# A two-layer sequence-model trunk: input handed over transposed too, the state-space input made channel by channel, its matrices and phases on VectorE

## What is computed

```python
h = x @ w_in
cq, ckv, k_rope, g_mla, u, g_s5 = split(h, (256, 128, 32, 512, 256, 256))
o_mla = mla_attention(cq, ckv, k_rope, pos, ...) * silu(g_mla)
o_s5 = s5_layer(u, ...) * silu(g_s5)
x = layer_norm(alpha * x + concat(o_mla, o_s5) @ w_out)
```

## Time and profile before

| | us |
|---|---|
| runs | 980.0, 981.01, 981.46 |
| median | 981.01 |
| profiled execution, span from first to last instruction | 978.8 |
| TensorE busy (matmul) in the span | 935.0 |
| VectorE, ScalarE, GpSimd busy | 457.3, 274.2, 275.9 |
| start of the first transposition of latents (cT) | 188.87 |

### The profile page before, as it was taken

How to read it: one execution, slowest core, us unless ns; L and a number is a source line. 1 busy time by engine, 2 the same in 40 slices (tenths; PEclk the granted TensorE clock), 3 DMA queues, 4 the chain that set the end, 5 groups by cost and what they waited for, 6 DMA issues and landing times. The chain is left out here.

```text
span 978.8 us, 12195 instructions
## 1 busy us (share of the span) xinstructions
PE 935.0 (96%) x4568; PEld 733.2 (75%) x4568; DVE 457.3 (47%) x764; ACT 274.2 (28%) x532; POOL 275.9 (28%) x278
## 2 busy tenths in 40 slices
PE   7997999799999999999999999999999999999995
PEld 5787899757677777784445477888888888888884
DVE  4539459993566569854443042310000023655453
ACT  4330510365333333431111344400110215222120
POOL 2018008433111110052344323013333343034233
PEclk9998999899999999999999899999999999999998
DMA  6501110233000000043221211011101233112111
GB/s 215 115 10 27 31 33 11 65 69 132 1 2 1 1 2 1 1 130 107 86 86 57 95 43 44 1 54 54 44 11 43 54 129 108 44 44 77 54 44 65
DMA packets 38874, 53.54 MB, mean 55 GB/s; under 512 B 15232, under 2 KB 24704, under 8 KB 38800
## 3 DMA queue, kind: packets, MB, share of 16 engines
q1 hardware_dynamic: 38816, 52.76, 17.6%
HBM read 42.72 MB, written 8.39 MB: 52 GB/s over the span
## 5 line engine op out<-in xcount | busy, mean ns | idle before, releaser
L1555 DVE SCALAR_TENSOR_TENSOR w_out_lo<-w_out_raw,gla_c,w_out_hi 128x1024 fp32r<-128x1024 f32 x8 | 10.3, 1285 | 161.9 <-ACT w_out_hi L1180 161.8
L1868 PEld LDWEIGHTS psum<-V,probT 128*128 128x128 f32 x576 | 69.3, 192 | 11.7 <-issue 8.1
L1868 PE MATMUL psum<-V,probT 128*128 128x64 f32 x576 | 74.4, 275 | 0.3 <-DVE rot L1502 0.3
L1727 PE MATMUL psum<-kT,qTt 96*128 96x512 f32 (+3 forms) x192 | 72.4, 487 | 0.0
L1112 ACT ACTIVATE prob<-psum,negmax 128x128 f32<-128x128 f32 (+7 forms) x64 | 47.4, 741 | 81.7 <-DVE negmax L1457 71.2
L1457 DVE TENSOR_REDUCE negmax<-psum 128x1 f32<-128x128 f32 (+7 forms) x64 | 48.5, 757 | 29.0 <-PE psum L1731 27.5
L1622 PE MATMUL psum<-w_out,OT 128*128 128x512 f32 x128 | 57.6, 593 | 0.0
L1622 PE MATMUL psum<-x1T_hi,wqk_hi 128*128 128x512 f32 x128 | 51.3, 401 | 0.0
L1622 PE MATMUL psum<-x1T_hi,wqk_lo 128*128 128x512 f32 x128 | 50.8, 397 | 0.0
L1622 PE MATMUL psum<-x1T_lo,wqk_hi 128*128 128x512 f32 x128 | 50.8, 397 | 0.0
L1622 PE MATMUL psum<-w_out_hi,Y1T_hi 128*128 128x512 f32 x128 | 50.6, 395 | 0.0
(11 more groups left out here) (365 smaller groups left out, 2115.9 us busy)
## 6 DMA issues: line engine op xcount, KB each, us to landing
x_ring<-x_dram SPq DMA_DIRECT2D x8, 512.0 KB, 5.4
wqk_raw<-odd_w_in_dram SPq DMA_DIRECT2D x8, 512.0 KB, 5.3
x_res<-x_dram SPq DMA_DIRECT2D x8, 512.0 KB, 3.4
x_scratch<-zn SPq DMA_DIRECT2D x8, 512.0 KB, 2.7
wv_raw<-odd_w_in_dram SPq DMA_DIRECT2D x16, 256.0 KB, 2.7
wg_raw<-odd_w_in_dram SPq DMA_DIRECT2D x16, 256.0 KB, 2.6
w_out_raw<-odd_w_out_dram SPq DMA_DIRECT2D x4, 1024.0 KB, 5.1
V<-x_scratch SPq DMA_DIRECT2D x8, 512.0 KB, 4.0
```

What stands on the lines that cost most here:

```text
L1555: step(vec.scalar_tensor_tensor(w_out1[2][:, k, :], w_out1[0][:, k, :], gla_c[:, 4 + k % 2:5 + k % 2], w_out1[1][:, k, :].bitcast(F32), AL ...
L1727: mm = pe.matmul(psum[:, slot + part, 0:c1 - c0], qTt[:, i % 2, h, :], kT[:, h, c0:c1], start=True, stop=not diag, skip_group_check=diag)
L1868: mm = pe.matmul(bank("o", i)[:, h * VD:(h + 1) * VD], lhsT, rhs, start=(k == 0), stop=(k == len(pairs) - 1))
```

## The change

- The host hands x over a second time as features by tokens (`x_cols`), and the small parameters in the layouts in which they are used (`pos_cols`, `vec_cols`, `s5_rows`, `s5_skip`). TensorE's transpositions of x, "par" and "crow" are gone; x is loaded in eight feature rows of 512 KB (the first in two halves), each split by ScalarE and VectorE in SBUF.
- "ug" becomes two blocks of 256 columns, "u" and "gs", one after the other. u is made channel-major, with 128 weight columns stationary and 512 tokens moving, as gs was. ScalarE copies it out by position t, two DMAs store it to a DRAM scratch tensor, and eight DMAs read it back as UT. SyncE waits for the store between them.
- Both halves of `phases` are run by VectorE, right after the first latents slices; ScalarE's sines come before slices 3 to 7 of "ina". VectorE makes NX and N2 itself, after the keys' rotation. GpSimd has none of this any more.
- VectorE's and ScalarE's lists are reordered to suit; the banks' ring no longer has par, crow and UT.

The diff, cut to its core:

```diff
-        wug = [split_pair(f"wug{s}", o, [P, 512]) for s, o in enumerate((D6, D6 + 1024, D3, D3 + 1024))]
-        xT_lo_parts = [at(f"xT_lo{n}", o, [P, b - a, S], F32R) for n, (a, b, o) in enumerate(
-            ((0, 2, RB + 7424), (2, 4, D4), (4, 7, D2), (7, 8, RB + 9472)))]
-        xT_lo = [t[:, k, :] for t in xT_lo_parts for k in range(t.shape[1])]
+        wu = [split_pair(f"wu{s}", D6 + 512 * s, [P, W5]) for s in range(4)]
+        wgs = [split_pair(f"wgs{s}", D3 + 512 * s, [P, W5]) for s in range(4)]
+        xT_at = (RB + 7424, RB + 8448, D4, D4 + 1024, D2, D2 + 1024, D2 + 2048, RB + 9472)
+        xT_raw = [at(f"xT_raw{k}", o, [P, S]) for k, o in enumerate(xT_at)]
...
+            ("rows", [P, 3 * G + 4 * G * GS], F32), ("dts", [P, 3, G], F32), ("dti", [P, G], I32),
...
+            ("u_rows", [P, 2, LC, NC5], F32),
...
+        u_dram = nc.dram_tensor("u_scratch", [W5, LC, NC5], F32, kind="Internal")
+        u_chunks = u_dram.ap() if not isinstance(u_dram, bass.AP) else u_dram
...
-        EARLY = 3
-        X_LAG = 2
-        for i in range(NT + X_LAG):
-            if i < NT:
-                plan.give(("xT", i, 0), 6 if i < NT - 1 else 7)
-                plan.give(("xT", i, 1), 7)
-            if i >= X_LAG:
-                plan.give(("gate0", i - X_LAG), i - X_LAG)
-        ring("par")
-        ring("crow")
+        for i in range(NT):
+            ring("gate0", i)
         for i in range(NT):
             ring("ina", i)
-        for j in range(4):
-            ring("inu", j)
+        for m in range(2):
+            for n in range(2):
+                ring("inu", m, n)
         for m in range(2):
             for n in range(2):
                 ring("ings", m, n)
         def middle_steps():
-            for q in range(4):
-                yield "UT", q
             for i in range(NT):
                 yield "cT", i
...
+            def small():
+                sp.dma_start(rows[:, :], s5_rows).then_inc(s5_loaded, 16)
+                sp.dma_start(Dt[:, :], s5_skip).then_inc(skip_loaded, 16)
+                sp.dma_start(pos_i[:, :], pos_cols).then_inc(small_loaded, 16)
+                sp.dma_start(vecs[:, :], vec_cols).then_inc(small_loaded, 16)
                 sp.dma_start(gk2[:, :], gla_w_gk2[0]).then_inc(small_loaded, 16)
...
-            for i in range(NT):
-                if i >= 4:
-                    plan.filled(sp, ("xT", i - 4, 1))
-                sp.dma_start(x_ring[:, i % 4, :], x[0, i * P:(i + 1) * P, :]).then_inc(x_loaded[i % 4], 16)
-                if i < EARLY:
-                    slice_load("gate0", i)
-                if i == 3:
-                    parameters()
-            for n in range(EARLY, 7):
-                plan.filled(sp, ("xT", n + 1, 1))
-                slice_load("gate0", n)
-            matrices()
+            for k in range(KD):
+                if k < 7:
+                    slice_load("gate0", k)
+                for half in range(2 if k == 0 else 1):
+                    s = slice(half * 512, (half + 1) * 512 if k == 0 else S)
+                    sp.dma_start(xT_raw[k][:, s], x_cols[k * P:(k + 1) * P, s]).then_inc(x_loaded[k + half if k == 0 else k + 1], 16)
+                if k == 2:
+                    small()
+            slice_load("gate0", 7)
             for n in range(3):
                 slice_load("ina", n)
-            vectors()
-            slice_load("gate0", 7)
-            for n in range(2):
-                slice_load("ug", n)
+            for n in range(4):
+                slice_load("u", n)
             for n in range(3, KD):
                 slice_load("ina", n)
             await_slice(sp, "ina", KD - 1)
-            for n in range(2, KD):
-                slice_load("ug", n)
-            await_slice(sp, "ug", KD - 1)
+            for n in range(4):
+                slice_load("gs", n)
+            for n in range(4, KD):
+                slice_load("u", n)
+            for m in range(2):
+                for n in range(2):
+                    plan.drained(sp, ("inu", m, n))
+                sp.dma_start(u_chunks[m * P:(m + 1) * P, :, :], u_rows[:, m, :, :]).then_inc(u_stored, 16)
+            slice_load("gs", 4)
+            sp.wait_ge(u_stored, 32)
+            for t in range(LC):
+                sp.dma_start(UT[t * GS:(t + 1) * GS, :, :],
+                             u_chunks[:, t, :].rearrange("(g h) c -> h g c", g=G)).then_inc(u_turned, 16)
+            for n in range(5, KD):
+                slice_load("gs", n)
+            await_slice(sp, "gs", KD - 1)
...
-            pool.wait_ge(s5_turns_set, 1)
-            phases(pool, step, 0, rot[:, :, :].rearrange("p a b -> p (a b)")[:, 0:8 * NTAB])
-            pool.wait_ge(s5_powers_set, 1)
-            for q in range(4):
-                matrix_part(pool, step, rot[:, 1:3, :].rearrange("p a b -> p (a b)")[:, 0:4 * (LC + 1) * GS], q, NX,
-                            LC + 1, LR[:, :, :], CA, LI[:, :, :], CB, ALU.subtract, s5_nx_set)
-            for q in range(4):
-                matrix_part(pool, step, rot[:, 2, :], q, N2, LC, LR[:, :, 1:LC + 1], CB, LI[:, :, 1:LC + 1], CA,
-                            ALU.add, s5_n2_set)
...
-            for i in range(NT):
+            for k in range(KD):
+                if k < 7:
+                    slice_hi("gate0", k)
                 for half in range(2):
-                    plan.filled(act, ("xT", i, half))
-                    step(act.activation(xT_hi[:, 4 * half:4 * half + 4, i * P:(i + 1) * P],
-                                        bank("xT", i, half).rearrange("p (k t) -> p k t", k=4), ACT.Copy), xT_hi_set)
-                if i < EARLY:
-                    slice_hi("gate0", i)
-            for n in range(EARLY, 6):
-                slice_hi("gate0", n)
+                    s = slice(half * 512, (half + 1) * 512)
+                    act.wait_ge(x_loaded[half if k == 0 else k + 1], 16)
+                    step(act.activation(xT_hi[:, k, s], xT_raw[k][:, s], ACT.Copy), xT_hi_set)
+            slice_hi("gate0", 7)
             for n in range(3):
                 slice_hi("ina", n)
-            for n in range(6, KD):
-                slice_hi("gate0", n)
+            for n in range(4):
+                slice_hi("u", n)
             for i in range(NT):
                 plan.filled(act, ("gate0", i))
...
+            act.wait_ge(s5_phase_set, 2)
+            step(act.activation(tabB[:, :, :], tabA[:, :, :], ACT.Sin, scale=-2 * PI_BELOW))
+            step(act.activation(tabA[:, :, :], tabA[:, :, :], ACT.Sin, scale=PI_BELOW), s5_sin_set)
...
+            for i in range(NT):
                 squares(act, step, i)
-            slice_hi("ug", 2)
-            for i in range(4, NT):
-                squares(act, step, i)
-            slice_hi("ug", 3)
             step(act.activation(stat[:, 16:24], stat[:, 0:8], ACT.Sqrt, bias=eps[:, 1:2], scale=1.0 / RQ))
             step(act.activation(stat[:, 24:32], stat[:, 8:16], ACT.Sqrt, bias=eps[:, 1:2], scale=1.0 / RKV),
                  squares_done)
+            for n in range(4):
+                slice_hi("gs", n)
             for n in range(4, KD):
-                slice_hi("ug", n)
-            for j in range(4):
-                plan.filled(act, ("inu", j))
-                step.frees(act.activation(U[:, :, 2 * j:2 * j + 2, :],
-                                          bank("inu", j).rearrange("p (t g h) -> p g t h", t=2, g=G), ACT.Copy),
-                           ("inu", j))
+                slice_hi("u", n)
+            for m in range(2):
+                for n in range(2):
+                    plan.filled(act, ("inu", m, n))
+                    step.frees(act.activation(u_rows[:, m, :, n * NC5 // 2:(n + 1) * NC5 // 2],
+                                              bank("inu", m, n).rearrange("p (c t) -> p t c", t=LC), ACT.Copy),
+                               ("inu", m, n))
+            for n in range(4, KD):
+                slice_hi("gs", n)
...
+            beside = {2: time_steps, 3: turns_of_steps, 4: magnitudes}
+            for k in range(KD):
+                if k < 7:
+                    slice_lo("gate0", k)
+                x_lo(k)
+                if k in beside:
+                    beside[k]()
+            slice_lo("gate0", 7)
             for n in range(3):
                 slice_lo("ina", n)
...
+            for half in range(2):
+                phases(vec, step, 8 * half, rot[:, :, :].rearrange("p a b -> p (a b)")[:, 0:8 * NTAB])
+            step(vec.tensor_scalar(CA, CA, sign[:, 1:2], None, ALU.mult))
+            for n in range(4):
+                slice_lo("u", n)
...
+            def make_nx(q):
+                matrix_part(vec, step, rot[:, 1:3, :].rearrange("p a b -> p (a b)")[:, 0:4 * (LC + 1) * GS], q, NX,
+                            LC + 1, LR[:, :, :], CA, LI[:, :, :], CB, ALU.subtract, s5_nx_set)
+            def make_n2(q):
+                matrix_part(vec, step, rot[:, 2, :], q, N2, LC, LR[:, :, 1:LC + 1], CB, LI[:, :, 1:LC + 1], CA,
```

(84 more changed lines are left out.)

275 lines of the change are left out of this document (103 added, 172 removed).

## The result

The changed kernel takes 926.13 us (median of 4 runs, 923.94 to 926.6) against 981.24 for the kernel before (4 runs, 980.0 to 981.74): a ratio of 0.944, 95% interval 0.943 to 0.946, or 55.1 us less. The forecast was 925. The profiled execution took 926.22 with a span of 924.5, so the time around the span is 1.7 us, where the prediction had put 2.2.

A forecast was written before the change was run, and what follows sets the result against it. TensorE, busy 96% of the span, bounds the kernel, with VectorE's sum meeting it before cT. 53.9 us less up to cT plus 2.0 after, 55.9 off 981.0, gives 925; range 919 to 934, chance 0.68.

The forecast's parts named there:

- u channel by channel: u stage on TensorE: 12 products of 512 columns instead of 24 of 256, 2.75 instead of 5.70 us a slice, 24 us less.
- rival of 949: u products keep their time because columns alone count, so the edit saves nothing there: 949 us, chance 0.01.
- Start: Without x's transpositions, TensorE's first product at 5.9 us, twelve slow products, gate products to 51.8, where the latents begin.
- Latents: Latents' projection: 192 products of 0.19 us, end 88.3; 8.4 us of waits and 3.5 after them go, 0.5 kept.
- The cover that the text called thin: Latents: after ScalarE's two sines slice 3 is split near 64, wanted at 65.4, a margin of 1 to 2 us.
- u and gs: Both stages on TensorE: 22 us each, end 132.3, plus 2 us of small waits: 134.3.
- The sum by VectorE: Up to cT: VectorE starts at 96.1, 35.7 us of instructions without pause to 131.8, last gs slice 2.75: 134.6.
- Bounce: u's DRAM store and read-back: done by 126, v wants it about 144; delays gs slice 5, costing one microsecond, bounds 0 and 9.
- signs that the prediction had listed as wrong: VectorE over 0.5 us per 256 elements, TensorE waiting on gs 5-7 behind a DMA, latents' clock 0.5, cT after 145.
- VectorE's price: Subtraction-sized VectorE instruction of 256 elements: 0.43 us with GpSimd idle; rival that slow rows are its own: 992 us, chance 0.03.
- After cT: Turned bank ring: 2.9 us less from kp's start to y, 0.9 more as first scores share banks with yT; net -2.0.
- Everything from the attention on is untouched: From the attention to the kernel's end: no change in time beyond the net -2.0 before it.

The follow-up runs named there:

- all three edits: Changed kernel with gs 5-7 loads before u's reads, M's last four steps and latents' halves earlier, u's slice 4 split ahead of gs 0-3: 919.41 us.
- second order of banks: Version with all three edits, the five banks that kp and vp take in turn reordered to 7, 4, 5, 6, 0: 919.4 us.
- the ring turned back: Changed kernel with four turns of the PSUM bank ring passed over before cT, so later jobs have the banks of the kernel before: 929.12 us.
- loads first: Changed kernel with SyncE issuing the loads of gs slices 5 to 7 before it waits for the stored u and reads it back: 924.67 us.
- M early: Changed kernel with the last four steps of M moved into VectorE's pause while ScalarE takes the squares: 925.29 us.
- latents forward: Changed kernel with latents' slice 3 split on ScalarE before the long sines and low halves from slice 4 on one place earlier on VectorE: 925.94 us.
- all of u cut: Changed kernel with all eight u slices as 24 products of 256 columns, the 512 moving tokens cut into 256 + 256: 930.44 us.
- GpSimd at work again: Changed kernel with the 24 instructions that make NX and N2 given back to GpSimd, beside VectorE: 948.05 us.

## Why the prediction was right, and where not

- **u channel by channel, 24 us:** right in size (slices of 2.74 us, 22.6 us in all with 0.5 of waits), wrong in its reason. The prediction reads "12 of them instead of 24", and takes 0.238 for 256 columns as the price of a product of that size. The runs show 0.12 for that size; 0.238 is the price of a stationary operand read with a stride of eight floats. The row was right and could not tell count, size and stride apart, because in the kernel before they came together: the reason failed, and it was luck that the sum did not need it. The rival of 949 failed because the stride went, not because columns don't count.
- **Start:** 6.17 for 5.9, the latents at 51.53 for 51.8; the slow start ended at 9.72, after eight products instead of twelve. (The 45 small instructions at 0.35 would be 16 us, not 12; both fit in the 25.)
- **Latents:** the step that failed is "I keep 0.5" for stalls: 2.5 was measured. Nor is the 0.5 in the sum: 88.3 is 51.8 and 36.5, the products alone. The cover that the text called thin was thinner: ScalarE's sines ran to 64.9 and slice 3's low half came at 65.63, slice 4's, behind the doubling of the table as named, at 71.94. Moving both forward took the waits away.
- **u and gs:** "2 us of small waits" were 2.7 (0.5 and 2.2), and the total of 47.1 stands beside 46.7. But "From here VectorE has no pause" failed: it stood 1.73 us for slice 5. The sum by VectorE explains where cT went: the start was 98.1 for 96.1 (2.0 late, with the latents), the pause added 1.7, the instructions took 35.0 instead of 35.7 (0.43, 0.76 and 0.69 each, as priced), and so the last low half was done at 134.85 for 131.8.
- **Bounce:** priced at one microsecond, and its removal gave 1.3 at cT, at the place that was named: slice 5 behind the eight reads, 128.6 for "near 127". Its parts were off and cancelled, which is luck: issuing the eight took 3.8 us, not 7; the slowest took 8.0 to land, not 3.5. This wait is one of the signs that the prediction had listed as wrong (TensorE waiting on gs slices 5 to 7 with a DMA behind it); of its signs for right, stalls under 2 us in the latents did not come either.
- **VectorE's price:** 0.43 undisturbed, as taken, and 1.16 to 1.40 with GpSimd beside it, as the rows said.
- **After cT:** 2.87 less up to y and 0.85 more up to glu, for 2.9 and 0.9.
- **"Everything from the attention on is untouched":** not quite. At glu the kernel was 3.1 us behind the forecast, at the end 1.6 in span: the second layer's queries and keys took 107.9 us (481.7 to 589.6) instead of 109.4 (534.4 to 643.8), with no instruction changed. That is the luck of the last section, and without it the forecast would have been 2.6 off instead of 1.1.
- **What no run isolates:** up to cT, 13.8 us came from the stage ahead of the latents (13.5 forecast), 9.1 from the latents (11.9) and 28.0 from u and gs, with u's transposition (28.4). The price of u's stride and of NX and N2 beside GpSimd were put to the test; the host's transposition and the phases' move are read from the timelines alone.

## What to carry to other kernels

Before a price per instruction is carried over to a new form, list what else changes with the form: here count, width and stride changed together, and only a run that varied one at a time showed that the stride of the stationary operand was what cost. When two engines arrive at the same time by the sum, the gain of any one edit is what is left until the next of them; look for all of them and take them together (1.3, 1.0 and 1.0 us alone, 6.4 together at cT). A store and read-back in DRAM cost nothing here by its own latency (the last read was issued at 120.3 us, the slowest landed in 8.0, and v began at 146.9), and 1.3 us by the loads that queued behind it: put those that are wanted first ahead of it.

## What the runs showed that was not expected

TensorE's granted clock made differences of one to three microseconds between traces in stages that the kernels share. In the attention one set of queries waits 1.09 us for the same VectorE copy, some 15 us after the first transposition of probabilities, in the kernel before and in the others alike. Here it is in the version with all three edits, and in the one with the second order of banks (there with two rows of the table by stage, granted clock behind the busy times):

```profile
203.47 1.56 PE L1585 MATMUL psum<-w_uq,cT 128*128 128x384 f32 x4 [1.09 <-DVE qTt L1414]
```

```profile
200.50:202.50 2.00, 0.91 (x7) 0.67 (x7) 1.90 (x4) 0.00 (x0) 0.00 (x0) 0.94 0.03 8
202.50:204.50 2.00, 2.00 (x4) 1.09 (x5) 0.59 (x2) 0.00 (x0) 0.00 (x0) 0.50 0.00 0
...
202.26 2.93 PE L1585 MATMUL psum<-w_uq,cT 128*128 128x384 f32 x4 [1.09 <-DVE qTt L1414]
```

The same four products after the same pause take 1.56 us in the one and 2.93 in the other, where the granted clock is 0.50 (1.2 GHz). From the first to the last transposition of probabilities it is 187.4 us in the eight traces where the clock stays up (among them the kernel before, the change, the ring turned back, all three edits) and 189.1 to 189.6 in the six where it falls (loads first, M early, latents forward, the second order of banks, all of u cut, GpSimd at work again). The instructions ahead of the pause are the same in both; what decides it was not isolated. The second layer's queries and keys vary in the same way: 109.4 us at a mean granted clock of 0.95 (the kernel before), 107.9 at 0.97 (the change), 106.3 at 0.98 (M early).

Each kernel has one trace, so these differences need not belong to the kernel. The mean granted clock of a whole execution varies within one kernel too: with all of u cut, one execution had 0.993 and took 926.73 us, the three others 0.989 and 930.31 to 931.06. Between all three edits (0.993 in all five executions) and the second order of banks (0.991 or 0.992 in all five) it does differ by kernel.

Longer pauses give no rule either. Those of 2.3 to 2.6 us before the first queries were followed by slow products in each of the three kernels that had them (4.54, 4.31 and 4.54 us instead of 2.74), and the 3.07 us in gs as well. But with M early, gs has a pause as long and keeps a granted clock of 1.00 after it (the next products start 0.23 apart):

```profile
128.72 0.50 PE L1620 MATMUL psum<-xT_hi,wgs_hi 128*128 128x512 f32 x1 [2.52 <-DVE wgs_lo L1212]
```

The same holds for the 3.11 us in the latents with GpSimd at work, shown above, and for the 1.3 us before kp. So a saving of a microsecond is read at the next fixed point of the trace, not from the time of the whole kernel, and a total that moves by 1.7 us is by itself no evidence for or against it.
